# A decoder step: 512-column moving operands in the expert tables, sample tokens' expert rows fetched by index, gates kept in another DRAM order

## The chip, the cores and the metric

The kernel runs on one core of one Trainium2 chip. The core has TensorE (PE, whose weight loads are shown apart as PEld), VectorE (DVE), ScalarE (ACT), GpSimd (POOL), SyncE (SP) and 16 DMA engines. The metric is the device time of one execution in microseconds (us); lower is better. Before the change three runs took 4409.46, 4419.07 and 4418.88 us, median 4418.88 us.

## The reference

A two-layer decoder trunk works on 520 tokens of width 1024 at once: 512 tokens of a prompt and 8 sample tokens (one new token each of 8 sequences). Layer 0 mixes tokens by a gated convolution and attention, layer 1 by a chunked spatial gate. The change is in what follows in each layer, an expert lookup (`_peer`). For each token, 8 heads pick 16 of 16,384 experts by two product keys, which gives 128 experts and 128 gates per token:

```python
q = (xf @ wq).reshape(n, PEER_HEADS, 2, PEER_DK // 2)
s = jnp.einsum('nhpd,hpkd->nhpk', q, keys)
top_s, top_i = lax.top_k(s, PEER_TOPK)               # 16 of 128, for two halves of the key
cand_s = top_s[:, :, 0, :, None] + top_s[:, :, 1, None, :]
cand_i = top_i[:, :, 0, :, None] * PEER_NKEYS + top_i[:, :, 1, None, :]
best_s, pos = lax.top_k(cand_s..., PEER_TOPK)        # 16 of 256
gate = jax.nn.softmax(best_s, axis=-1)
hi = jax.nn.gelu(jnp.einsum('bed,bd->be', jnp.take(u_tab, ei, axis=0), xi))
y  = jnp.einsum('be,bed->bd', gi * hi, jnp.take(v_tab, ei, axis=0))
```

An expert's number is 128 times a first index plus a second index. `u_tab` and `v_tab` have 16,384 rows of 1024 numbers each, 64 MB per table and layer. All numbers are fp32.

## The kernel before, in words

Activations lie with the features on the partitions: `xt`, `res` and the like are [128, 8, 520], feature block by feature block, with the 520 tokens side by side (columns 512 to 519 are the sample tokens).

The expert lookup (`peer`, on each engine a function of that name, called for layer 0 and layer 1) doesn't fetch rows. It multiplies all tokens by both whole tables and lets the gates, which are zero for experts that were not picked, select.

- **First table.** For each of 128 first indices a chunk of 128 experts' u rows (512 KB) is multiplied by all tokens: `chunk` on PE (line 1229; the matmul is line 1241). fp32 accuracy comes from splitting each operand into a rounded part and a remainder (`whi`, `wlo`, `xh`, `xl`, float32r), with three products for each of 8 feature blocks. The 520 columns are done in two matmuls of 260, so a chunk is 48 matmuls. SP loads a chunk into `wraw` (two slots), ACT rounds it (`whi`, line 570), POOL takes the remainder (`wlo`, line 547), PE multiplies, ACT applies the gelu (`hid`, line 696) and SP stores the 128x520 result to DRAM (`hidden`, line 414). The rounding of the next chunk of a slot stands behind the gelu of the present one on ACT, and the gelu waits until the store of that slot's result before has landed (`h_out`).
- **Gates.** Beside the first table the tokens are ranked, 104 at a time (5 token tiles, `topk` on DVE). A tile's gates are then spread out on PE: for groups of 4 tokens DVE builds two one-hot matrices (`one_hots`, lines 1196 and 1199) and PE multiplies them (`gate_group`, line 1434) to a 128x128 table of gates per token. ACT copies it into `gst` (line 710), and SP stores `gst` by half tiles of 52 tokens, each in four pieces of 832 KB (`store_gates`, line 421). `PLAN` says after how many pairs of chunks each tile's work comes, and whether one or two groups of tokens follow each chunk. In DRAM `gates` is [first index, second index, token], so a store writes runs of 52 numbers (208 bytes).
- **Second table.** For each of 32 groups of four first indices, and each of 8 feature blocks (v = 0 to 7), PE adds up `second_table` (line 1490, matmul line 1499): 4 first indices by 3 products by 2 halves, 24 matmuls of 260 columns. The moving operand is `wth`/`wtl`, the rounded part and the remainder of hidden times gate (`gated` on DVE, line 1052; `round_wt` on ACT, line 764; `split_wt` on DVE, line 1056). The weights are `vhi`/`vlo` (ACT line 757, DVE line 1043). DVE adds each result to `res` (`take_v`, line 1064). SP loads the v rows (line 399, four slots), hidden (line 428) and gates (line 429, 260 KB for each first index).

The order on each engine is written out by hand: program order with semaphores. SP issues all loads and stores of both tables from one queue, in the order of the code, and waits there for each one's condition.

The lines most spoken of are these:

```python
for h in range(2):                                              # chunk, line 1239
    mm = e.matmul(pstr[:, slot, h, 0:HALF], w[:, slot, k * P:(k + 1) * P], x[:, k, h * HALF:(h + 1) * HALF], ...)
for h in range(2):                                              # second_table, line 1498
    mm = e.matmul(aux[:, 2 * (v % 2) + h, 0:HALF], w[:, v % 4, j * P:(j + 1) * P], x[:, par, j, h * HALF:(h + 1) * HALF], ...)
```

Of the kernel before, what the change touches and what calls it, by code (L numbers as in the profile page):

```python
# [30 lines left out]
P = 128  # L31
# [21 lines left out]
SUB = 4  # L53
GROUP = 4
# [5 lines left out]
GROUPS = TT // SUB  # L60
EXP_AT = 17
# [19 lines left out]

SMP = {"operands": 0, "bias": 1, "keys": 2, "max": 17, "exp": 19, "norm": 19, "turn": 20, "turned": 20, "values": 21}
# [21 lines left out]
class Steps:  # L104
# [10 lines left out]
    def settle(self):  # L115

        self.engine.wait_ge(self.sem, self.count)

# [10 lines left out]
def trunk(nc, i, o):  # L129
    with ExitStack() as ctx:  # L130
# [81 lines left out]
        choice_end = used[0]  # L212

# [4 lines left out]
        wth = place("wth", [P, 2, GROUP, N], F32R)  # L218
        wtl = place("wtl", [P, 2, GROUP, N], F32R)
        gc = place("gc", [P, GROUP, N], F32)  # L220
        hl = place("hl", [P, GROUP, N], F32)
        wt = place("wt", [P, 2, N], F32)

        hid = place("hid", [P, 2, N], F32, max(used[0], choice_end))
        used[0] = max(used[0], choice_end) + 2 * 4 * N
# [29 lines left out]
        g_in = [sem(f"g_in{n}") for n in range(4)]  # L255
# [69 lines left out]
        v_taken = sem("v_taken")  # L325

# [47 lines left out]
        def _(e):  # L374
# [26 lines left out]
            def peer_tables(layer):  # L401
# [15 lines left out]
                def store_gates(half, part):  # L417

                    n = P // PIECES
                    e.wait_ge(gate_taken, (half + 1 + layer * NT * 2) * subs)  # L420
                    e.dma_start(gates[layer][part * n:(part + 1) * n, :, half * GH:(half + 1) * GH].rearrange("a b n -> b a n"),
                                gst[:, half % 2, part * n:(part + 1) * n, :]).then_inc(gates_out[half % 2], 16)

                def load_h(g, j):
# [4 lines left out]
                    e.dma_start(gc[:, j, :], gates[layer][bass.ds(g * GROUP + j, 1)].rearrange("a p n -> p (a n)")).then_inc(g_in[j], 16)  # L429
# [12 lines left out]
                while pair < P // 2:  # L442
# [4 lines left out]
                    if pair == P // 2 - 3:  # L447

                        for par in range(2):
                            e.wait_ge(gates_out[par], 16 * PIECES * NT * (layer + 1))  # L450
                        for j in range(GROUP):
                            load_h(0, j)
                        for v in range(4):
                            load_v(layer, 0, v)
                    store_h(pair)
# [10 lines left out]
                def period(g, more):  # L466
# [6 lines left out]
                period(0, True)  # L473
                with e.Fori(1, NG - 1) as g:
                    period(g, True)
                period(NG - 1, False)
# [21 lines left out]
        def _(e):  # L498
# [37 lines left out]
            def peer(layer):  # L536
# [6 lines left out]
                with e.Fori(1, P // 2) as p:  # L543
                    for slot in range(2):
# [3 lines left out]
                                        ALU.subtract).then_inc(u_lo, 1)  # L548

# [14 lines left out]
        def _(e):  # L564
# [119 lines left out]
            def peer(layer):  # L684
# [6 lines left out]
                def hidden_one(pair, slot):  # L691
# [4 lines left out]
                    e.activation(halves(hid[:, slot, :]), pstr[:, slot, :, 0:HALF], ACT.Gelu_apprx_tanh).then_inc(chunk_taken, 1)  # L696
# [7 lines left out]
                def take_gates(tt, n):  # L704
# [4 lines left out]
                    e.wait_ge(gate_done, tt * GROUPS + (n + 1))  # L709
# [55 lines left out]

                def period(g, par, more):
                    for v in range(8):
# [4 lines left out]
                        elif more:  # L772
                            round_v(g + 1, v - 6)

# [5 lines left out]
                period(0, 0, True)  # L780
                with e.Fori(0, NG // 2 - 1) as q:
# [28 lines left out]
        def _(e):  # L810
# [213 lines left out]
            def peer(layer):  # L1024
# [3 lines left out]

                for w in range(NT + 1):
                    tt = w + layer * NT  # L1030
                    ranking = topk(tt, Steps(e, topk_step, tt * per), per) if w < NT else iter(())
                    if w:
                        e.wait_ge(pick_taken, tt)
                        for n in range(GROUPS):
                            one_hots((tt - 1) * GROUPS + n, n % 2, n * SUB)
# [9 lines left out]
                def gated(g, j):  # L1045
# [602 lines left out]
```

## Time and profile before

| what | value |
|---|---|
| three runs, median | 4409.46, 4419.07, 4418.88 us; 4418.88 us |
| span of the profiled execution, first to last instruction | 4402.0 us |
| PE busy | 4151.5 us, 94% |
| PEld busy | 3973.3 us, 90% |
| DVE, ACT, POOL busy | 2675.8 us (61%), 1465.7 us (33%), 765.7 us (17%) |
| first-table matmuls, line 1241 | 16,512 (some 12,288 of them in the two first tables) |
| second-table matmuls, line 1499 | 12,288 |
| DMA | 633.66 MB, 144 GB/s on average; 359,736 of 582,347 packets are under 512 bytes |

The page gives no time of the profiled execution beside its span; the runs are 7.5 to 17.1 us longer than it. "Busy" of PE is not work at its peak, since matmuls overlap and their ends are modelled; their starts tell the pace. "Granted clock" is the share of TensorE's full clock in a stretch; 1.00 is 2.4 GHz and 0.50 is 1.2 GHz. In time the execution is: attention and its projections up to about 490 us, the first table of layer 0 to about 1547 us (its gates from 655 us), the second table to about 2295 us, the spatial gate to about 2570 us, and the two tables of layer 1 to about 4373 us.

### The profile page before, as it was taken

To read this page: it belongs to the slowest core of one execution; us is meant where nothing else is said; L and a number is where in the kernel's file an instruction comes from. 1 tells how busy PE (TensorE), PEld (TensorE's weight loads), DVE (VectorE), ACT (ScalarE), POOL (GpSimd) and SP (SyncE) were. 2 spreads that over 40 slices of the span, in tenths; PEclk is the share of its full clock that TensorE was granted. 3 is DMA by queue.
4 is the path that set the end of the run, shared out by engine and by line. 5 is a ranking of instruction groups with operands and counts; after the bars stand their busy time and mean duration, and the time that the engine had idled before them with its cause. 6 is when DMAs were issued, how large, how long until landed. Compare 5 with 4: busy or idle time off the path is not lost.

```text
span 4402.0 us, 85855 instructions
## 1 busy us (share of the span) xinstructions
PE 4151.5 (94%) x32404; PEld 3973.3 (90%) x32404; DVE 2675.8 (61%) x5472; ACT 1465.7 (33%) x2084; POOL 765.7 (17%) x430
## 2 busy tenths in 40 slices
PE   8889999999898899999999999999999989999998
PEld 8635899989898899999999789999999889999998
DVE  2332368787786266666653336868787626666665
ACT  3221333434434322222224233433343432222223
POOL 4111123333232300000001012333333320000000
PEclk9989999999999999999999799999999999999999
DMA  4444235766777955555542023576696786555553
GB/s 120 131 128 139 77 113 133 145 132 139 141 139 137 182 183 184 183 184 184 183 134 74 28 77 113 135 144 135 141 147 146 132 174 193 182 182 183 184 184 112
DMA packets 582347, 633.66 MB, mean 144 GB/s; under 512 B 359736, under 2 KB 359864, under 8 KB 581584
## 3 DMA queue, kind: packets, MB, share of 16 engines
q1 hardware_dynamic: 573760, 608.77, 55.0%
q0 software_dynamic: 8464, 23.38, 1.8%
q8 instruction: 62, 1.02, 0.1%
q14 instruction: 61, 0.50, 0.0%
HBM read 491.36 MB, written 140.66 MB: 144 GB/s over the span
## 4 chain that ended last, share of the span: by engine, by line
PE 49%; issue 39%; POOL 8%; ACT 2%; DVE 2%; DMA 1%; POOLq 0%; SPq 0%; ACTq 0%; DVEq 0%
PE aux L1499 33%; PE pstr L1241 9%; POOL wlo L547 8%; PE pstr L1366 1%; PE pstr L1386 1%; PE aux L1284 1%; PE pstr L1339 1%; PE aux L1546 1%; PE aux L1545 0%; PE aux L1275 0%; DVE rstd L847 0%; PE aux L1319 0%; PE aux L1329 0%; ACT xt L604 0%; PE pstr L1275 0%
## 5 line engine op out<-in xcount | busy, mean ns | idle before, releaser
L1241 PE MATMUL pstr<-xh,whi 128*128 128x260 f32 x5504 | 1155.3, 292 | 114.1 <-POOL wlo L547 86.4
L1241 PE MATMUL pstr<-xh,wlo 128*128 128x260 f32 x5504 | 1124.2, 286 | 0.0
L1241 PE MATMUL pstr<-xl,whi 128*128 128x260 f32 x5504 | 1122.6, 286 | 0.0
L1241 PEld LDWEIGHTS pstr<-xh,whi 128*128 128x128 f32 x5504 | 868.7, 193 | 124.8 <-issue 85.5
L547 POOL TENSOR_TENSOR wlo<-wraw,whi 128x1024 fp32r<-128x1024 f32 x252 | 633.4, 2515 | 1460.6 <-ACT whi L570 1459.1
L1241 PEld LDWEIGHTS pstr<-xl,whi 128*128 128x128 f32 x5504 | 867.6, 193 | 0.0
L1241 PEld LDWEIGHTS pstr<-xh,wlo 128*128 128x128 f32 x5504 | 864.9, 192 | 0.0
L1499 PE MATMUL aux<-wth,vhi 128*128 128x260 f32 x4096 | 827.0, 283 | 7.5 <-DVE res L1064 7.5
L1499 PE MATMUL aux<-wth,vlo 128*128 128x260 f32 x4096 | 826.8, 284 | 0.0
L1499 PE MATMUL aux<-wtl,vhi 128*128 128x260 f32 x4096 | 825.5, 283 | 0.0
L1499 PEld LDWEIGHTS aux<-wth,vhi 128*128 128x128 f32 x4096 | 633.4, 189 | 8.5 <-DVE vlo L1043 7.9
L1199 DVE TENSOR_SCALAR oh<-cst,pickt 128x128 f32<-128x128 f32 x1040 | 637.7, 674 | 0.0
L1499 PEld LDWEIGHTS aux<-wth,vlo 128*128 128x128 f32 x4096 | 632.8, 189 | 0.0
L1499 PEld LDWEIGHTS aux<-wtl,vhi 128*128 128x128 f32 x4096 | 631.2, 189 | 0.0
L1043 DVE TENSOR_TENSOR vlo<-vraw,vhi 128x512 fp32r<-128x512 f32 x512 | 352.1, 688 | 308.9 <-ACT vhi L757 308.9
L764 ACT ACTIVATE wth<-wt 128x520 fp32r<-128x520 f32 x256 | 163.2, 638 | 1025.0 <-DVE wt L1052 1025.0
L696 ACT ACTIVATE hid<-pstr 128x520 f32<-128x520 f32 x256 | 156.5, 611 | 1038.5 <-PE pstr L1241 794.0
L1064 DVE TENSOR_TENSOR res<-res,aux 128x520 f32<-128x520 f32 x512 | 354.6, 693 | 209.1 <-PE aux L1499 209.1
L1196 DVE TENSOR_TENSOR oh<-cst,pickt 128x512 f32<-128x512 f32 x260 | 201.2, 774 | 395.5 <-PE aux L1434 318.3
L570 ACT ACTIVATE whi<-wraw 128x1024 fp32r<-128x1024 f32 x344 | 361.5, 1051 | 122.4 <-PE pstr L1241 86.7
L1434 PE MATMUL aux<-oh,oh 128*128 128x128 f32 x2080 | 282.1, 284 | 41.1 <-ACT gst L710 27.7
L710 ACT ACTIVATE gst<-aux 128x512 f32<-128x512 f32 x260 | 312.7, 1240 | 15.1 <-PE aux L1434 14.9
(194 smaller groups left out, 2906.5 us busy)
## 6 DMA issues: line engine op xcount, KB each, us to landing
wraw<-in_u SPq DMA_DIRECT2D x256, 512.0 KB, 3.8
vraw<-in_v SPq DMA_DIRECT2D x512, 256.0 KB, 2.9
hidden<-hid SPq DMA_DIRECT2D x256, 260.0 KB, 2.2
gates<-gst SPq DMA_DIRECT2D x80, 832.0 KB, 18.5
hl<-hidden SPq DMA_DIRECT2D x256, 260.0 KB, 2.7
gc<-gates SPq DMA_DIRECT2D x256, 260.0 KB, 3.9
wraw<-in_w SPq DMA_DIRECT2D x88, 512.0 KB, 3.5
kv<-in_ck SPq DMA_DIRECT2D x32, 256.0 KB, 3.1
```

The lines of the kernel that those rows point to most:

```text
L547: e.tensor_tensor(wlo[:, slot, :], wraw[:, slot, :], whi[:, slot, :].bitcast(F32), ALU.subtract).then_inc(u_lo, 1)
L570: e.activation(whi[:, slot, :], wraw[:, slot, :], ACT.Copy).then_inc(w_hi, 1)
L696: e.activation(halves(hid[:, slot, :]), pstr[:, slot, :, 0:HALF], ACT.Gelu_apprx_tanh).then_inc(chunk_taken, 1)
L710: e.activation(gst[:, half % 2, :, n % subs * SUB:(n % subs + 1) * SUB].rearrange("p a n -> p n a"), aux[:, n % 2, :].rearrange("p (n a) - ...
L764: e.activation(wth[:, par, j, :], wt[:, j % 2, :], ACT.Copy).then_inc(wt_hi, 1)
L1043: e.tensor_tensor(vlo[:, v % 4, :], vraw[:, v % 4, :], vhi[:, v % 4, :].bitcast(F32), ALU.subtract).then_inc(v_lo, 1)
L1064: e.tensor_tensor(r, r, aux[:, 2 * (v % 2):2 * (v % 2) + 2, 0:HALF], ALU.add).then_inc(v_taken, 1)
L1196: e.tensor_tensor(oh2[:, slot], spread(c(IOTA), 1, shape), spread(pickt[:, 1, at:at + SUB], 2, shape), ALU.is_equal).then_inc(oh_ready, 1)
L1199: e.tensor_scalar(oh1[:, slot, r, :], c(IOTA), pickt[:, 0, at + r:at + r + 1], pickt[:, 2, at + r:at + r + 1], ALU.is_equal, ALU.mult).the ...
L1241: mm = e.matmul(pstr[:, slot, h, 0:HALF], w[:, slot, k * P:(k + 1) * P], x[:, k, h * HALF:(h + 1) * HALF], start=k == 0 and w is whi and x ...
L1434: mm = e.matmul(aux[:, slot, r * P:(r + 1) * P], oh2[:, slot, r, :], oh1[:, slot, r, :], start=True, stop=True)
L1499: mm = e.matmul(aux[:, 2 * (v % 2) + h, 0:HALF], w[:, v % 4, j * P:(j + 1) * P], x[:, par, j, h * HALF:(h + 1) * HALF], start=j == 0 and w ...
```

## The change

The tables' matmuls take the 512 prompt tokens alone, in one matmul of 512 columns in place of two of 260. In the first table a result fills one PSUM bank (`pstr[:, slot, 0, :]`), in the second table `aux[:, v % 2, :]`. `hid`, `hl`, `wt`, `wth`, `wtl` and `hidden` shrink from 520 to 512 columns.

The 8 sample tokens get their experts' rows by index. At the end of the ranking DVE writes the expert numbers and gates of these tokens (`sample_list`). POOL then fetches, for one token after the other, the 128 u rows (one row per partition, 512 KB) and later the 128 v rows, by indirect DMA into a ring of four buffers `rows`. In the groups g = 1 and 2 of the second table PE spreads a token's activations over all partitions (`sample_spread`) and DVE multiplies them with the rows and adds up (`sample_dot`). In the groups 3 and 4 PE multiplies the v rows with gate times gelu (`sample_values`), and DVE adds the sum to `res` (`sample_add`). Groups 0 to 4 are therefore written out, and the loop over the rest starts later.

`gates` in DRAM becomes [half tile, second index, first index, token]: a store writes, for each partition, 32 first indices by 52 tokens in one run (6,656 bytes). The gates of four first indices are loaded at once, double-buffered by group, in 10 runs of 832 bytes per partition, and `gated` becomes two multiplications, of 468 and of 44 columns.

```diff
-        gates = [nc.dram_tensor(f"gates{n}", (P, P, N), F32, kind="Internal").ap() for n in range(DEPTH)]
-        hidden = [nc.dram_tensor(f"hidden{n}", (P, P, N), F32, kind="Internal").ap() for n in range(DEPTH)]
+        gates = [nc.dram_tensor(f"gates{n}", (2 * NT, P, P, GH), F32, kind="Internal").ap() for n in range(DEPTH)]
+        hidden = [nc.dram_tensor(f"hidden{n}", (P, P, SEQ), F32, kind="Internal").ap() for n in range(DEPTH)]
...
-                    e.dma_start(gates[layer][part * n:(part + 1) * n, :, half * GH:(half + 1) * GH].rearrange("a b n -> b a n"),
-                                gst[:, half % 2, part * n:(part + 1) * n, :]).then_inc(gates_out[half % 2], 16)
+                    e.dma_start(gates[layer][half, :, part * n:(part + 1) * n, :].rearrange("b a n -> b (a n)"),
+                                gst[:, half % 2, part * n:(part + 1) * n, :].rearrange("b a n -> b (a n)")).then_inc(gates_out[half % 2], 16)
...
-                    e.dma_start(gc[:, j, :], gates[layer][bass.ds(g * GROUP + j, 1)].rearrange("a p n -> p (a n)")).then_inc(g_in[j], 16)
+                def load_gates(g, par):
+                    if layer or not isinstance(g, int) or g > 1:
+                        e.wait_ge(g_used, g * GROUP + (layer * P - GROUP))
+                    e.dma_start(gc[:, par, :, :], by_group[bass.ds(g, 1)].rearrange("a b h c -> b (a h) c")).then_inc(g_in[par], 16)
...
+                for j in range(2 * DEC):
+                    table, t = (i["ur"], j) if j < DEC else (i["vr"], j - DEC)
+                    if RING <= j < RING + DEC:
+                        e.wait_ge(s_dot, layer * DEC + j - RING + 1)
+                    elif j >= RING + DEC:
+                        e.wait_ge(s_value, layer * DEC + j - RING - DEC + 1)
+                    e.indirect_dma_start(rows[:, j % RING, :], None, table,
+                                         bass.IndirectOffsetOnAxis(ap=s_id[:, t:t + 1], axis=0)).then_inc(rows_in[j % RING], 16)
...
+                def sample_dot(t):
+                    e.wait_ge(rows_in[t % RING], 16 * (2 * DEC // RING * layer + t // RING + 1))
+                    e.wait_ge(s_spread, layer * DEC + t + 1)
+                    row = rows[:, t % RING, :]
+                    e.scalar_tensor_tensor(row, row, 1.0, pstr[:, 0, :, :].rearrange("p a n -> p (a n)"), ALU.mult, ALU.mult,
+                                           accum_out=s_dots[:, t:t + 1]).then_inc(s_dot, 1)
...
+                        if first in C_U:
+                            mm = e.matmul(pstr[:, slot, 0, :], w[:, slot, k * P:(k + 1) * P], x[:, k, 0:SEQ],
+                                          start=k == 0 and w is whi and x is xh, stop=k == KB - 1 and w is wlo)
+                            continue
...
-                            for h in range(2):
-                                mm = e.matmul(aux[:, 2 * (v % 2) + h, 0:HALF], w[:, v % 4, j * P:(j + 1) * P],
-                                              x[:, par, j, h * HALF:(h + 1) * HALF],
+                            mm = e.matmul(aux[:, v % 2, :], w[:, v % 4, j * P:(j + 1) * P], x[:, par, j, :],
...
+                def sample_spread(t):
+                    if t == 0:
+                        e.wait_ge(s_rows, 3 * (layer + 1))
+                    if t or layer:
+                        e.wait_ge(s_dot, layer * DEC + t)
+                    for h in range(2):
+                        for n in range(2):
+                            mm = e.matmul(pstr[:, 0, h, :], pickr[:, t:t + 1].to_broadcast([DEC, P]), xr[:, n, h * 512:(h + 1) * 512],
+                                          start=n == 0, stop=n == 1)
+                    mm.then_inc(s_spread, 1)
+
+                def sample_values(t):
+                    if t == 0:
+                        e.wait_ge(s_weight, layer + 1)
+                    j = DEC + t
+                    e.wait_ge(rows_in[j % RING], 16 * (2 * DEC // RING * layer + j // RING + 1))
+                    for k in range(KB):
+                        at = k * DEC + t
+                        mm = e.matmul(aux[:, 2, at:at + 1], rows[:, j % RING, k * P:(k + 1) * P], s_w[:, t:t + 1], start=True, stop=True)
+                    mm.then_inc(s_value, 1)
...
+                        if DOTS_G <= g < DOTS_G + 2 and v % 2 == 0:
+                            sample_spread((g - DOTS_G) * 4 + v // 2)
+                        if g == VALS_G and v >= 2:
+                            sample_values(v - 2)
+                        if g == VALS_G + 1 and v < 2:
+                            sample_values(v + 6)
```

The next rows are SP's queue where a layer's first table ends and its second begins, before the change (`wraw` is a chunk of u, `hl` and `gc` the hidden values and gates of a first index, `vraw` a block of v rows).

```order
L421 DMA gates<-gst 128x32x52 x2
L414 DMA hidden<-hid 128x520 x2
L382 DMA wraw<-in_u 128x1024 x2
L428 DMA hl<-hidden 128x520
L429 DMA gc<-gates 128x520
...
L399 DMA vraw<-in_v 128x512 x4
L414 DMA hidden<-hid 128x520 x2
```

After the change the same place on SP reads:

```order
L452 DMA gates<-gst 128x1664 x2
L445 DMA hidden<-hid 128x512 x2
L413 DMA wraw<-in_u 128x1024 x2
L466 DMA gc<-gates 128x10x208
L459 DMA hl<-hidden 128x512 x4
L430 DMA vraw<-in_v 128x512 x4
L466 DMA gc<-gates 128x10x208
L445 DMA hidden<-hid 128x512 x2
```

The stores of gates stand where they stood, with one run per partition; two loads of four first indices' gates take the place of four loads of one, the second of them ahead of the store of hidden values.

The next rows are DVE in the second table before the change, two feature blocks of a group (`wt` is hidden times gate, `vlo` a remainder of v, `res` the sum that takes PE's result).

```order
L1064 TENSOR_TENSOR res<-res,aux 128x520
L1052 TENSOR_TENSOR wt<-hl,gc 128x520
L1043 TENSOR_TENSOR vlo<-vraw,vhi 128x512
L1064 TENSOR_TENSOR res<-res,aux 128x520
L1056 TENSOR_TENSOR wtl<-wt,wth 128x520
L1043 TENSOR_TENSOR vlo<-vraw,vhi 128x512
```

After the change, in group 1:

```order
L1170 TENSOR_TENSOR res<-res,aux 128x512
L1155 TENSOR_TENSOR wt<-hl,gc 128x468
L1157 TENSOR_TENSOR wt<-hl,gc 128x44
L1144 TENSOR_TENSOR vlo<-vraw,vhi 128x512
L1170 TENSOR_TENSOR res<-res,aux 128x512
L1115 SCALAR_TENSOR_TENSOR rows,s_dots<-rows,pstr 128x1024
L1162 TENSOR_TENSOR wtl<-wt,wth 128x512
L1144 TENSOR_TENSOR vlo<-vraw,vhi 128x512
```

The product with the gates is split in two in every group; the instruction of line 1115 stands behind every second feature block of groups 1 and 2 only.

## Rows read from the trace of the kernel before

**Rows 1.** Page, the chain that ended last, by line.

```profile
PE aux L1499 33%; PE pstr L1241 9%; POOL wlo L547 8%; PE pstr L1366 1%; PE pstr L1386 1%; PE aux L1284 1%; PE pstr L1339 1%; PE aux L1546 1%; PE aux L1545 0%; PE aux L1275 0%; DVE rstd L847 0%; PE aux L1319 0%; PE aux L1329 0%; ACT xt L604 0%; PE pstr L1275 0%
```

**Rows 2.** Stretches: busy us (count) by engine, granted clock, DMA share, GB/s.

```profile
1800.00:1900.00 100.00, 100.00 (x834) 100.00 (x834) 66.40 (x104) 28.64 (x52) 0.00 (x0) 1.00 0.58 186
...
883.24:949.44 66.20, 66.20 (x563) 66.20 (x561) 55.37 (x133) 24.57 (x28) 21.91 (x9) 1.00 0.67 135
...
655.19:1556.41 901.22, 828.31 (x6718) 823.58 (x6717) 632.73 (x1474) 347.27 (x397) 288.45 (x114) 0.96 0.73 143
...
2744.80:3638.33 893.53, 824.47 (x6718) 819.89 (x6717) 623.17 (x1474) 346.92 (x397) 284.78 (x114) 0.96 0.73 144
...
1135.09:1182.18 47.09, 36.23 (x250) 35.38 (x249) 38.28 (x53) 19.15 (x20) 13.14 (x5) 0.86 0.55 111
```

**Rows 3.** Timeline of PE at half clock: start, us, what, count.

```profile
977.73 0.64 PE L1241 MATMUL pstr<-xh,whi 128*128 128x260 f32 x2
...
978.16 0.64 PE L1241 MATMUL pstr<-xl,whi 128*128 128x260 f32 x2
```

**Rows 4.** Timeline of PEld, fp32 matmuls of 512 columns, full clock granted.

```profile
250.11 0.14 PEld L1366 LDWEIGHTS pstr<-kv,qd 128*64 128x64 f32 x1 [0.29 <-issue]
...
250.54 0.14 PEld L1366 LDWEIGHTS pstr<-kv,qd 128*64 128x64 f32 x1 [0.29 <-issue]
```

**Rows 5.** Timeline of PE, fp32 matmuls of 260 columns, each in two passes.

```profile
2294.68 2.79 PE L1275 MATMUL pstr<-res,cst 128*128 128x260 f32 x12
```

**Rows 6.** Waits of PE in the whole span: us in total, times, longest.

```profile
PE pstr L1241 <- POOL wlo L547: 86.4, 22, 6.4
...
PE aux L1434 <- ACT gst L710: 27.7, 10, 4.2
...
PE aux L1434 <- DVE oh L1199: 13.2, 5, 4.8
```

**Rows 7.** Timeline of SP's queue at two stores of gates.

```profile
943.60 11.98 SPq L421 DMA_DIRECT2D gates<-gst  x2
```

**Rows 8.** Timeline of ACT and PE after it; idle before in brackets.

```profile
968.56 1.28 ACT L696 ACT_TABLE_LOAD   x1 [11.02 <-DMA hidden<-hid]
...
976.27 0.79 PE L1241 MATMUL pstr<-xh,whi 128*128 128x260 f32 x2 [6.37 <-POOL wlo L547]
```

**Rows 9.** DMA issues: count, KB each, median us to landing.

```profile
gates<-gst SPq DMA_DIRECT2D x80, 832.0 KB, 18.5
...
hidden<-hid SPq DMA_DIRECT2D x256, 260.0 KB, 2.2
...
vraw<-in_v SPq DMA_DIRECT2D x512, 256.0 KB, 2.9
...
kv<-in_cv POOLq DMA_DIRECT2D x32, 256.0 KB, 3.2
```

**Rows 10.** Timeline of DVE and ACT over two feature blocks of the second table.

```profile
1702.42 0.69 DVE L1064 TENSOR_TENSOR res<-res,aux 128x520 f32<-128x520 f32 x1 [0.75 <-PE aux L1499]
...
1703.04 0.69 DVE L1052 TENSOR_TENSOR wt<-hl,gc 128x520 f32<-128x520 f32 x1
...
1703.76 0.64 ACT L764 ACTIVATE wth<-wt 128x520 fp32r<-128x520 f32 x1 [4.11 <-DVE wt L1052]
...
1704.31 1.14 ACT L757 ACTIVATE vhi<-vraw 128x512 fp32r<-128x512 f32 x2
...
1704.96 0.69 DVE L1043 TENSOR_TENSOR vlo<-vraw,vhi 128x512 fp32r<-128x512 f32 x1 [1.23 <-ACT vhi L757]
...
1705.56 0.69 DVE L1064 TENSOR_TENSOR res<-res,aux 128x520 f32<-128x520 f32 x1
...
1706.17 0.69 DVE L1056 TENSOR_TENSOR wtl<-wt,wth 128x520 fp32r<-128x520 f32 x1
```

**Rows 11.** Timeline of PE, fp32 matmuls with 4 columns and full weights.

```profile
400.17 1.95 PE L1415 MATMUL aux<-cab,om 128*128 128x4 f32 x16 [1.37 <-DVE om L1014]
```

**Rows 12.** Costliest groups: a DVE pass over 1024 columns that reads PSUM.

```profile
L1014 DVE TENSOR_TENSOR om<-pstr,cab 128x1024 f32<-128x1024 f32 x1 | 1.2, 1225 | 29.0 <-PE pstr L1386 29.0
```

More of the change, by code:

```diff
@@ L254, in trunk @@
         v_in = [sem(f"v_in{n}") for n in range(4)]
-        g_in = [sem(f"g_in{n}") for n in range(4)]
+        g_in = [sem(f"g_in{n}") for n in range(2)]
         h_out = [sem(f"h_out{n}") for n in range(2)]
@@ L325, in trunk @@
         v_taken = sem("v_taken")
+        s_listed = sem("s_listed")
+        s_turned = sem("s_turned")
+        s_rows = sem("s_rows")
+        rows_in = [sem(f"rows_in{n}") for n in range(RING)]
+        s_spread = sem("s_spread")
+        s_dot = sem("s_dot")
+        s_gelu = sem("s_gelu")
+        s_weight = sem("s_weight")
+        s_value = sem("s_value")
         ws_masked = sem("ws_masked")
@@ L471, in period @@
                             load_h(g + 1, v // 2)
[L473 to L476, printed above, removed]
+                        if gates_too and v == 1:
+                            load_gates(g + 2, par)
+                period(0, 0, True)
+                with e.Fori(0, NG // 2 - 2) as q:
+                    period(q * 2 + 1, 1, True)
+                    period(q * 2 + 2, 0, True)
+                period(NG - 3, 1, True)
+                period(NG - 2, 0, True, False)
+                period(NG - 1, 1, False, False)
             load_stage(C_AB, N_AB, i["w"], 0, None)
@@ L548, in peer @@
                                         ALU.subtract).then_inc(u_lo, 1)
+                for par in range(2):
+                    e.wait_ge(gates_out[par], 16 * PIECES * NT * (layer + 1))
+                e.wait_ge(s_listed, layer + 1)
+                for j in range(2 * DEC):
[6 more added lines that the diff above has]
+                                         bass.IndirectOffsetOnAxis(ap=s_id[:, t:t + 1], axis=0)).then_inc(rows_in[j % RING], 16)
             peer(0)
@@ L779, in peer @@
                 hidden_pair(P // 2 - 1)
-                period(0, 0, True)
-                with e.Fori(0, NG // 2 - 1) as q:
+                for g in range(VALS_G + 2):
+                    period(g, g % 2, True)
+                with e.Fori((VALS_G + 1) // 2, NG // 2 - 1) as q:
                     period(q * 2 + 1, 1, True)
@@ L1506, in period @@
                         second_table(g, v, par)
-                period(0, 0)
-                with e.Fori(0, NG // 2 - 1) as q:
+                        if not isinstance(g, int):
+                            continue
+                        if (g, v) == (0, 4):
+                            sample_turn()
+                        if DOTS_G <= g < DOTS_G + 2 and v % 2 == 0:
+                            sample_spread((g - DOTS_G) * 4 + v // 2)
[3 more added lines that the diff above has]
+                            sample_values(v + 6)
+                for g in range(VALS_G + 2):
+                    period(g, g % 2)
+                with e.Fori((VALS_G + 1) // 2, NG // 2 - 1) as q:
                     period(q * 2 + 1, 1)
```

124 lines of the change are left out of this document (96 added, 28 removed).

## The prediction, made before the changed kernel ran

> **What bounds the kernel now.** I read the chain of waits first: the second table's matmuls alone are 33% of the span on it, and the first table's, of which the profile puts most down to "issue", make up the larger part of the rest [rows 1]. So PE is the engine to look at, and the stretches tell how. In the second table PE is busy all the time at a granted clock of 1.00 and starts 834 matmuls of 260 columns in 100 us, 119.9 ns each, while DVE is busy 66% and DMA 58% [rows 2]. That is PE's own pace. In the first table a clean stretch of ten groups gives 563 matmul records in 66.20 us, 117.6 ns each. But the two whole stretches with gates hold 6718 records in 901.22 and 893.53 us at a mean clock of 0.96 [rows 2]. At the clean pace 6718 records are 790 us, so 111 and 104 us, 215 in all, are waits and the half clock that follows them.
>
> The waits are mostly of one kind: 86.4 us in 22 waits for POOL's remainder of u, and 27.7 us for ACT's copy of gates [rows 6]. One of them, step by step: SP is held 11.98 us by two stores of gates [rows 7]; the store of hidden values stands behind them, ACT sits idle 11.02 us until it has landed, the rounding of the next chunk stands behind that on ACT, and PE idles 6.37 us for POOL [rows 8]. A store of gates takes 18.5 us to land where 260 KB of hidden values take 2.2 us [rows 9].
>
> **One matmul of 512 columns for two of 260.** 260 columns at 2.4 GHz are 108.3 ns, and the measured pace is 119.9. At half clock two starts lie 0.43 us after the two before [rows 3], which is 217 ns each, 260 columns at 1.2 GHz with nothing on top. So the extra 11.6 ns are no fixed price of an instruction at every clock. Two explanations are left: something beside the stream (the load of 128 weight columns) takes about 120 ns and no longer hides, or the stream of float32r at full clock can't go faster. fp32 records of 512 columns start 430 ns apart [rows 4], which is two cycles a column at 2.4 GHz (426.7 ns) and 3 ns, and 12 of 260 columns (216.7 ns of stream, full weights) take 2.79 us, about 219 ns apart once the last one's 382 ns, its group's mean in the trace, are taken off [rows 5]. In both, the weights hide behind a stream of over 200 ns and 2 to 3 ns are left. A float32r matmul of 512 columns streams 213.3 ns with the same weights. I take 216 ns. The ends are 213.3 (nothing on top) and 235.8 (the pace per column of now, 119.9 x 512 / 260); I choose the value nearest to the fp32 rows, since their stream is as long and hides the same load.
>
> The Trainium skill, "TensorE: Matmul & The Clock Gate", section "Back-to-back issue gap", gives N / 2.4 + 2.5 ns for a warm matmul, an estimate of 216 at 512 columns. By the same rule 260 columns would take 111, and the row says 120; the miss of 9 ns is why I don't hold the 216 for certain. The page also names about 131 ns per matmul at N = 512 as sustained; 512 columns at 2.4 GHz are 213 ns, and no run here shows such a pace.
>
> First table: 256 chunks go from 48 x 119.9 = 5.76 us to 24 x 216 = 5.18, saving 0.57 us each, 146 us. Second table: 512 tiles go from 24 x 119.9 = 2.88 to 12 x 216 = 2.59, saving 0.285 each, 146 us. Sum 292 us.
>
> Is PE still last in the second table? DVE and ACT pass a chain through two feature blocks: sum into res at 1702.42, product with the gates, ACT's two roundings, remainder of v, next sum at 1705.56, which is 3.14 us; then three more DVE steps of 0.61 us, 1.83 [rows 10]. That is 4.97 us against 5.76 of PE. After the change the product is two instructions (I add 0.14 us for the second start, taking both ends of 0 to 0.35), and 8 fewer columns in four steps take 0.03 off: 5.08 against 2 x 2.59 = 5.18. PE stays last by 0.1 us. With 0.35 the chain would be 5.29 and cost 0.11 x 256 = 28 us. DMA moves the same 4.2 MB or so per group in 20.7 us in place of 23, so a share of 58% becomes about 65%; SP's loads run four blocks ahead and land in 2.9 us [rows 9], so I count nothing for the shorter runs of the gates' loads.
>
> **Gates in one run per partition.** A store goes from 4096 runs of 208 bytes to 128 runs of 6,656 bytes. Loads with 128 runs of 2,048 bytes land in 2.9 us [rows 9]; four times the bytes should land in 4 to 8 us and hold SP for less than a microsecond. Then the hidden store is no longer late, and neither are ACT, POOL and PE. What is late next is DVE. In the clean stretch it is busy 55.37 of 66.20 us, 5.54 per group [rows 2]; PE's cycle falls from 6.62 to 5.18 + 0.87 = 6.05, so DVE just keeps up. At a token tile's end, where the ranking's large steps fall, it doesn't: from 1135.09 to 1182.18 DVE is busy 38.28 us for eight groups and four chunks [rows 2], which PE would do in 4 x 5.18 + 8 x 0.87 = 27.7. Two of a layer's tiles have such an end (two groups after each chunk): 10.6 us and some 2 us of half clock each, 25 us. I give the two other tiles 7 us together, and 12 us to the boundaries between tiles and to the step into the second table, where hidden values still have to land. So 44 us a layer stay of 107, and 127 us go in both layers. The ends: nothing goes (0) and all goes (215).
>
> **The fetched sample tokens.** PE gains work in the second table, per layer: 16 transposes at about 0.11 us, 32 matmuls of 512 columns at 0.216, and 64 fp32 products with one column, two passes each. Sixteen such records with 4 columns take 1.95 us with the last one's tail [rows 11], 0.113 apart, so 128 take 14.5 us. Sum 1.8 + 6.9 + 14.5 = 23 us, 46 in both layers. DVE gains eight passes over 1024 columns, which take about 1.2 us [rows 12]; in groups 1 and 2 its chain is then 6.3 us for two blocks against PE's 5.18 + 0.87, 0.25 x 8 = 2 us a layer. I add 1 us a layer for the first wait of ACT and PE on each other: 6 us in all. The 32 fetches of 512 KB are costed at nothing on PE: the first four of a layer are issued before the second table starts, and the later ones have four blocks of lead, 4 x (2.59 + 1.8) = 17.6 us in groups 3 and 4. POOL's loads of 256 KB took 3.2 us to land [rows 9]; twice the bytes, 6.4 us. If that cover is gone PE waits, see below. From 0 to 17 us a fetch are the bounds I see.
>
> **Sum.** 292 + 127 - 52 = 367 us. The profiled execution's span of 4402.0 becomes 4035. The median of the runs is 16.9 us over that span, so about 4052, and I forecast 4055 us.
>
> **The rivals.**
> Contention for weights (the 9 ns of excess stay on every matmul, 225 ns): 12,288 x 9 = 111 us less gain, 4165 us. For it speaks that the float32r pace of 119.9 is 9 ns over what fp32 shows on top of its stream; against it, that at 1.2 GHz there is no excess.
> The stream is the limit (235.8 ns): 243 us less; the longer chunks then give DVE back about 10, so 4290 us. For it: float32r reads a column per cycle, which no fp32 row does. Against: nothing but the fp32 rows, which read at half that rate.
> DVE's tile ends are hidden (it runs up to two groups ahead): up to 75 us more gain, 3980 us.
> The stores of gates stay slow, because 832 KB and not the 208-byte runs are what holds SP: the change doesn't do that part, 127 us less, 4180 us. Against it speaks that 512 KB of v rows as two loads land in a few us [rows 9].
> Slower than before: the fetches are exposed. POOL needs long for a fetch of 128 rows while DVE works, and PE stands in order at a product whose rows have not come. To eat 367 us the 32 fetches must each hold PE 11.5 us; with 17.6 us of lead, one would have to take 29 us from its release to its landing, and the time would be 4420 or more. POOL's loads at 3.2 us speak against it. The Trainium skill, "SBUF — State Buffer", section "Who interferes with whom", says that a DMA issued by GpSimd waits while DVE, in some of its modes, holds their shared port; its loads here ran while DVE was less busy than in the second table, so this row doesn't refute it.
>
> **How the numbers follow.** Forecast 0.55, its own range 4005 to 4130 (the chain's 28 us, half of the stalls' bounds, 219 ns for a matmul); contention 0.20; stream 0.10; DVE hidden 0.10; stores slow 0.02; fetches exposed 0.03. A range of 3985 to 4235 leaves out the stream, the exposed fetches and half of "DVE hidden", 0.18. A change below 0.3% (13 us) couldn't be told from none. All cases but the exposed fetches end far below 4406: faster 0.96, same 0.01, slower 0.03.
>
> **What would show it.** In the second table 463 records of 512 columns per 100 us (216 ns); 444 or 424 would be the rivals. No wait over 10 us of ACT for hidden values; waits for POOL gone but for a few us, and the longest waits of PE in the first table those for DVE's one-hots at the ends of the third and fourth token tile. Stores of gates landing under 8 us. A granted clock of 0.98 or more in the first tables. The fetches landing under 10 us, and no wait of PE for them. I would be wrong if the second table's tile took over 2.75 us, if PE still waited for POOL some 20 times, or if lines of the sample tokens cost PE over 40 us a layer.

## The result and the profile after

The changed kernel took 4198.13 us (median of 4 runs, 4193.99 to 4209.97), and the kernel before, on the same chip in the same session, 4414.17 us: ratio 0.9526, 95% interval 0.9503 to 0.9549. It is faster, as forecast, and its time lies in the range of 3985 to 4235 us, but 143 us above the 4055 us of the forecast. On another chip the gap was smaller: there the unedited change took 4199.09 us and the kernel before 4364.14 us, ratio 0.9631 (0.9606 to 0.9656). The change takes the same on both; it is the kernel before that differs.

The profiled execution of the change has a span of 4193.8 us against 4402.0, 208 us less. Its stretches, to be laid beside [rows 2] (columns as there):

```profile
1800.00:1900.00 100.00, 100.00 (x442) 82.84 (x441) 70.77 (x129) 31.04 (x54) 0.00 (x0) 1.00 0.59 190
...
644.85:1457.31 812.46, 792.92 (x3979) 664.45 (x3980) 638.75 (x1499) 347.69 (x398) 298.66 (x119) 0.99 0.48 162
2627.55:3440.28 812.73, 793.23 (x3980) 664.70 (x3980) 638.92 (x1499) 347.69 (x398) 298.30 (x119) 0.99 0.48 162
```

In the second table PE still has no gap and the clock is whole, but there are 442 matmuls in 100 us where I expected 463. The first table's stretch with gates fell from 901 and 894 us to 812 and 813, with the granted clock up from 0.96 to 0.99 and the DMA share down from 0.73 to 0.48. So the stalls went, and the matmuls are what came out dearer. Their starts say by how much; first the second table, then the first (start, us, instruction):

```profile
1799.80 0.39 PE L1617 MATMUL aux<-wth,vhi 128*128 128x512 f32 x1
...
1802.06 0.39 PE L1617 MATMUL aux<-wtl,vhi 128*128 128x512 f32 x1
```

```profile
663.11 0.40 PE L1356 MATMUL pstr<-xh,wlo 128*128 128x512 f32 x1
...
665.91 0.39 PE L1356 MATMUL pstr<-xh,wlo 128*128 128x512 f32 x1
```

The first pair is ten matmuls apart, 2.26 us. Over a whole table the starts stand 226.6 ns apart. The second pair is twelve apart, 2.80 us, 233 ns; the mean spacing within the first tables' chunks is 232.6. The forecast had 216 for both. All other signs that the prediction named came as expected. PE's waits (total, times, longest; beside [rows 6]):

```profile
PE aux L1553 <- DVE oh L1314: 19.2, 8, 4.0
...
PE pstr L1356 <- POOL wlo L591: 11.9, 6, 3.1
...
PE aux L1617 <- DVE res L1170: 7.1, 3, 3.5
...
PE aux L1553 <- ACT gst L767: 0.9, 4, 0.2
```

The 22 waits for POOL are 6, none over 3.1 us, and DVE's one-hots now lead. DMA issues and SP's queue, beside [rows 7, 9]:

```profile
gates<-gst SPq DMA_DIRECT2D x80, 832.0 KB, 7.1
gc<-gates SPq DMA_DIRECT2D x64, 1040.0 KB, 5.5
hidden<-hid SPq DMA_DIRECT2D x256, 256.0 KB, 2.1
...
rows<-in_ur,s_id POOLq DMA_INDIRECT x16, 5.3
rows<-in_vr,s_id POOLq DMA_INDIRECT x16, 4.6
```

```profile
906.18 0.90 SPq L452 DMA_DIRECT2D gates<-gst  x2
```

Two stores hold SP 0.90 us instead of 11.98, and a store lands in 7.1 us instead of 18.5; it is still 832 KB, so the rival that the size holds SP falls. The fetches of sample rows land in 5.3 and 4.6 us, and no wait of PE names them.

### The profile page after: what moved, and what is told of

Same layout as the page of the kernel before. It is cut to its first block and busy times, and to the rows that moved or that the text cites. A ratio compares the mean times of both kernels' runs of the same rounds, so it can differ in the third digit from the quotient of the medians.

```text
span 4193.8 us, 61594 instructions
## 1 busy us (share of the span) xinstructions
PE 4040.5 (96%) x20468; PEld 3334.9 (80%) x20468; DVE 2710.7 (65%) x5770; ACT 1478.5 (35%) x2092; POOL 814.5 (19%) x462
## 5 line engine op out<-in xcount | busy, mean ns | idle before, releaser
L1356 PE MATMUL pstr<-xh,whi 128*128 128x512 f32 x2048 | 832.7, 407 | 12.0 <-POOL wlo L591 11.9
L1356 PE MATMUL pstr<-xh,wlo 128*128 128x512 f32 x2048 | 814.9, 398 | 0.0
L1617 PE MATMUL aux<-wth,vhi 128*128 128x512 f32 x2048 | 805.0, 393 | 7.1 <-DVE res L1170 7.1
L1356 PE MATMUL pstr<-xl,whi 128*128 128x512 f32 x2048 | 809.8, 395 | 0.0
L1617 PE MATMUL aux<-wth,vlo 128*128 128x512 f32 x2048 | 799.1, 390 | 0.0
L1617 PE MATMUL aux<-wtl,vhi 128*128 128x512 f32 x2048 | 798.7, 390 | 0.0
L1356 PEld LDWEIGHTS pstr<-xh,whi 128*128 128x128 f32 x2048 | 388.7, 190 | 95.0 <-issue 15.1
L1356 PEld LDWEIGHTS pstr<-xh,wlo 128*128 128x128 f32 x2048 | 387.8, 189 | 92.1
L1356 PEld LDWEIGHTS pstr<-xl,whi 128*128 128x128 f32 x2048 | 388.9, 190 | 84.6
L1170 DVE TENSOR_TENSOR res<-res,aux 128x512 f32<-128x512 f32 x512 | 350.1, 684 | 135.1 <-PE aux L1617 133.3
```

The costliest lines, as they stand in the source:

```text
L1170: e.tensor_tensor(r, r, aux[:, v % 2, :], ALU.add).then_inc(v_taken, 1)
L1356: mm = e.matmul(pstr[:, slot, 0, :], w[:, slot, k * P:(k + 1) * P], x[:, k, 0:SEQ], start=k == 0 and w is whi and x is xh, stop=k == KB - ...
L1617: mm = e.matmul(aux[:, v % 2, :], w[:, v % 4, j * P:(j + 1) * P], x[:, par, j, :], start=j == 0 and w is vhi and x is wth, stop=j == GROUP ...
```

## The experiments

Times are medians. Several chips were used; the change took 4198 and 4199 us on the two where it ran unedited, and where two kernels are compared across chips, the text says so.

**The gates' layout alone**, on the kernel before, with 260-column matmuls and sample columns kept (stores shown; the loads, not shown, take four first indices at once):

```diff
-e.dma_start(gates[layer][part*n:(part+1)*n, :, half*GH:(half+1)*GH]..., gst[...])
+e.dma_start(gates[layer][half, :, part*n:(part+1)*n, :].rearrange("b a n -> b (a n)"), gst[...])
```

> The kernel before with only the gates' layout of the change (stores in one run per partition, loads for four first indices); 260-column matmuls and sample columns stay. Theory: the waits of PE that hang on the stores go, 127 us by the prediction, 135 to 140 us by what is left of the change's 208 us when 125 us of shorter matmuls and 50 to 57 us of sample work are taken out of it: 4275 to 4290 us, 0.968 to 0.971 of before. Rival (the stalls were bounded by PE's own pace and DVE, and the shorter matmuls gave what was gained): 80 us or less, 0.98 or above.

4266.51 us (4260.37 to 4269.57) against 4360.33 for the kernel before on that chip: 94 us less, 0.9784 (0.9755 to 0.9813). Its waits and landing:

```profile
PE aux L1448 <- DVE oh L1213: 23.9, 10, 3.8
...
PE pstr L1255 <- POOL wlo L560: 9.7, 6, 2.6
```

```profile
gates<-gst SPq DMA_DIRECT2D x80, 832.0 KB, 7.2
```

The ratio lies between the two bands and settles nothing, and the time is 9 us under the theory's 4275 to 4290: the kernel before is 54 us faster on this chip than where it was profiled, so the sums don't carry over. The mechanism is shown: with only the layout changed, the waits for POOL fall from 22 to 6 (and the next run, on this same chip, has 22 of them with the old layout).

**The reverse: the change with the old layout.**

```diff
-gates (2*NT, P, P, GH), gc per four first indices
+gates (P, P, N), gc[:, j, :] per first index, 0:SEQ
```

> The changed kernel with the gates' layout of before (208-byte runs, loads per first index), 512-column matmuls and fetched sample rows kept. Theory: PE waits for POOL come back, some 20 waits and 80 to 110 us, and the time is 4198 + 127 to 140 = 4325 to 4338 us, 0.980 to 0.983 of before. Rival (with fewer, longer matmuls a late store costs no more than before per store, but DVE's lag hides part of it): 4260 to 4290 us, 0.965 to 0.972.

4320.29 us (4310.18 to 4323.47), 121 us over the 4199.09 of the change on another chip, where the kernel before takes nearly as long (4364 us, here 4360). That is 5 us under the band of 4325 to 4338 us, and 0.990 of before, outside both bands.

```profile
PE pstr L1341 <- POOL wlo L581: 70.5, 22, 6.0
...
PE aux L1538 <- ACT gst L757: 16.5, 9, 3.0
```

```profile
929.41 10.53 SPq L452 DMA_DIRECT2D gates<-gst  x2
```

The 22 waits for POOL are back, 70.5 us where 80 to 110 were expected, with SP held for 10.53 us by two stores. With 512 columns the layout is worth 121 us, with 260 it was 94; that a shorter chunk leaves a late store less cover is my reading, and no run tests it. Turned round: without the layout, the wider matmuls and the fetched samples together gain only 40 us on this chip (4360.33 to 4320.29), so the gains of the two parts of the change don't simply add up.

**The change without the sample tokens' expert work.**

```diff
-sample_list() / indirect_dma_start(rows...) / sample_turn, _spread, _dot, _weights, _values, _add
```

> The changed kernel without the sample tokens' part of the expert tables (no fetch of rows, no dots, no products with the fetched rows, nothing added to the sample columns): their share of the output is left out. Theory: PE loses 16 transposes, 32 matmuls of 512 columns and 128 one-column records a layer, 25 us, and the few us of waits around them: 50 to 57 us in both layers, 4141 to 4148 us, 0.939 to 0.941 of before. Rival (the sample work stands where PE would have waited for DVE and ACT): 25 us or less, 0.946 or above.

4147.98 us (4146.10 to 4165.90): 51 us under the change (4199.09, another chip), against the 52 us of the prediction. The work is on the path at about its full price. Rows of the change show one of its pieces, 16 products with one column, and that the table's next matmul starts 1.71 us after the first of them, with no wait between:

```profile
3539.91 1.84 PE L1649 MATMUL aux<-s_w,rows 128*128 128x1 f32 x16
3541.62 0.48 PE L1617 MATMUL aux<-wth,vhi 128*128 128x512 f32 x1
```

**What makes a matmul of 512 columns cost 226.6 ns?** Two runs change one thing, or two, in each table:

```diff
 # first run: layer 0, both tables: 32 weight columns; layer 1: row 0 of x throughout, 384 columns
+mm = e.matmul(pstr[0:cols, ...], w[:, slot, k*P:k*P+cols], x[:, row, 0:SEQ], ...)
+mm = e.matmul(aux[0:cols, v%2, 0:n], w[:, v%4, j*P:j*P+cols], x[:, par, j, 0:n], ...)
 # second run: weight block 0 throughout, and row 0 in layer 1; second table 256 columns, then 64 partitions
+mm = e.matmul(pstr[:, slot, 0, :], w[:, slot, 0:P], x[:, row, 0:SEQ], ...)
+mm = e.matmul(aux[:, v%2, 0:n], w[0:rows_, v%4, j*P:(j+1)*P], x[0:rows_, par, j, 0:n], ...)
```

> The changed kernel; in layer 0 both tables use 32 weight columns in place of 128 (32 output features of 128 are computed), in layer 1 the first table's matmuls all read row 0 of x in place of row k, and the second table's stream 384 columns of 512. The outputs of the tables are partial by that. Theory (the load of 128 weight columns is what is left uncovered, 13 ns over the 213.3 of the stream): with 32 columns the spacing falls to 213 to 218 ns in both tables, the first table's extra 6 ns with it. Rival 1 (the stream pays by column): spacing stays 226.6 with 32 weight columns, 384 columns take 170 ns. Rival 2 (a fixed price of an instruction): stays with 32 weight columns, 384 columns take 160 + 13.3 = 173.3 ns. For the first table's 232.5 against 226.6: if the place of the moving row does it, row 0 throughout gives one even spacing in layer 1; if not, the pattern of 227 to 238 ns by position stays.

> The changed kernel; the first table's matmuls take weight block 0 throughout (layer 0), and weight block 0 with row 0 of x (layer 1); the second table streams 256 columns in layer 0, and in layer 1 contracts over 64 partitions of 128. The tables' outputs are partial by that. Rate by column: 256 columns take 113.3 ns; fixed price: 106.7 + 13.3 = 120; a weight load that no longer hides: about 120 as the 260-column matmuls of before. 64 partitions: a theory of reads from the buffer says less than 226.6, the others the same. First table: if weights' and row's addresses meet, the pattern is even in layer 1 and changed in layer 0; if it is the instruction's place in its chunk, it stays in both.

Starts in the second table. 32 weight columns and 512 streamed (ten apart, 2.32 us, 232 ns); 384 streamed (nine apart, 1.56 us, 173.3 ns), both of the first run:

```profile
1799.77 0.39 PE L1619 MATMUL aux<-wth,vhi 128*32 128x512 f32 x1
...
1802.09 0.39 PE L1619 MATMUL aux<-wtl,vhi 128*32 128x512 f32 x1
...
3899.74 0.34 PE L1619 MATMUL aux<-wth,vlo 128*128 128x384 f32 x1
...
3901.30 0.34 PE L1619 MATMUL aux<-wth,vlo 128*128 128x384 f32 x1
```

256 streamed (six apart, 0.72 us, 120 ns), and 512 over 64 partitions at half clock (six apart, 2.56 us, 426.7 ns), of the second run:

```profile
1802.74 0.28 PE L1619 MATMUL aux<-wtl,vhi 128*128 128x256 f32 x1
...
1803.46 0.28 PE L1619 MATMUL aux<-wtl,vhi 128*128 128x256 f32 x1
...
3899.72 0.62 PE L1619 MATMUL aux<-wth,vhi 64*128 64x512 f32 x1
...
3902.28 0.62 PE L1619 MATMUL aux<-wth,vhi 64*128 64x512 f32 x1
```

A quarter of the weight columns made nothing shorter, so the load of weights is not what stays uncovered. Over 1/2.4 ns a column, 256 columns have 13.3 ns on top, 384 have 13.3 and 512 have 13.3: a fixed price of each float32r matmul, neither a share per column nor a load that hides behind a longer stream. At half clock it is gone (512 / 1.2 is 426.7), as with the 260 columns of [rows 3]. The height doesn't matter either: in the first tiles with 64 partitions, still at full clock, the starts stood 226.7 ns apart. One figure doesn't fit to the nanosecond: the 260 columns of the kernel before had 11.6 ns on top, not 13.3, and no run shows why.

The second run is much longer, 4773.90 us, because of its last part:

```profile
3500.00:4100.00 600.00, 600.00 (x1463) 462.40 (x1463) 220.14 (x392) 92.13 (x167) 4.89 (x5) 0.50 0.32 104
```

With 64 of 128 partitions contracted the clock was granted at 0.50 for the whole of 600 us, while PE was busy throughout. It fell 13.6 us into the table and stayed there to the table's end. I hadn't expected that; it is told again below.

The same runs show the second table's floor. Where PE streams only 384 columns, PE waits for DVE, and DVE and ACT, which mostly wait for each other there, set the pace:

```profile
3700.00:3800.00 100.00, 85.76 (x468) 80.12 (x467) 73.19 (x137) 32.92 (x57) 0.00 (x0) 1.00 0.63 207
```

468 matmuls of 12 a tile in 100 us are 2.56 us a tile, 5.13 for two; the prediction worked out 5.08.

**Why the first table pays 6 ns more.** My first theory was the start of every other row of x at 32 bytes off a multiple of 64:

```diff
-xh = place("xh", [P, KB, N], F32R)
+xh = place("xh", [P, KB, N + 8], F32R)      # xl likewise
```

> The changed kernel with the rows of xh and xl padded from 2080 to 2112 bytes, so that every row starts at a multiple of 64 bytes as the second table's rows do. Theory (row starts): the first table's matmuls of 512 columns take 232.5 ns in place of the second table's 226.6 because every other row of x starts 32 bytes off; then both tables go at 226.6, 6144 x 5.9 ns = 36 us less, 0.944 of before against 0.953 of the change. Rival (the place of the weights, or of the instruction in its chunk): the spacing in a chunk stays 227 to 238 ns by position, mean 232.5, and the time stays at 0.953. The 32-column matmuls of the other stages read the same rows and should show the same sign.

4203.75 us (4196.65 to 4206.02), no gain. Twelve matmuls of its first table still take 2.78 us, 232 ns:

```profile
661.40 0.39 PE L1357 MATMUL pstr<-xh,wlo 128*128 128x512 f32 x1
...
664.18 0.40 PE L1357 MATMUL pstr<-xh,wlo 128*128 128x512 f32 x1
```

That theory fell. But the pattern of short and long spacings within a chunk had moved, so the rows' places did matter. In the two runs above the pattern was the same within a nanosecond with weight block 0 throughout (mean 232.6), and with row 0 throughout it settled at 227 after ten matmuls (mean 228.3). So it is the moving rows, not which weight block is loaded. The next run sets the distance between them:

```diff
+at = k * 512 if first == C_U[0] else k % 7 * 576          # 2048 or 2304 bytes, before 2080
+mm = e.matmul(pstr[...], w[...], x[:].rearrange("p a n -> p (a n)")[:, at:at + SEQ], ...)
+at = j % 3 * 520 if layer == 0 else j * SEQ               # second table: 2080 bytes, before 2048
```

> The changed kernel with the moving rows taken at other distances in the same tensors: in the first table the k-th row starts at 2048 k bytes in layer 0 and at 2304 (k mod 7) bytes in layer 1, in place of 2080 k; in layer 0's second table the rows start at 2080 (j mod 3) bytes in place of 2048 j. The tables' values are wrong by that. Theory (the distance from one moving row to the next makes the first table's spacing uneven): at 2048 bytes layer 0's first table goes at 227 ns from the tenth matmul of a chunk on, as with row 0 throughout, mean 227 to 228 against 232; layer 0's second table becomes uneven, 229 to 234 in place of 226.6; 2304 bytes tell which distances are even. Rival (the chunk's start behind the gate group's products of 128 columns, and 24 matmuls in place of 12, make it): nothing changes in either table.

In layer 0's first table twelve spacings of a chunk's later half now take 2.72 us, 226.7 ns, and the mean is 228.3 in both layers, so with either distance; in the second table of layer 0, with 2080 bytes, ten take 2.32 us, 232 ns:

```profile
665.42 0.39 PE L1357 MATMUL pstr<-xh,wlo 128*128 128x512 f32 x1
...
668.14 0.40 PE L1357 MATMUL pstr<-xh,wlo 128*128 128x512 f32 x1
...
1799.69 0.39 PE L1619 MATMUL aux<-wtl,vhi 128*128 128x512 f32 x1
...
1802.01 0.40 PE L1619 MATMUL aux<-wth,vlo 128*128 128x512 f32 x1
```

The tables swapped their prices with their distances. That is shown. The rival keeps a small part: behind a gate group's products of 128 columns the first ten spacings of a chunk stay uneven, 224 to 236 ns, even at 2048 and 2304 bytes, while a chunk with no group before it goes at 227 from its start. The run as a whole took 4196.14 us (one run), hardly less: layer 0's second table lost about 14 us by its spacing, the first tables won about 26, and the waits for DVE's one-hots grew from 19.2 to 25.4 us.

**A better order of the gates.** The longest waits left beside the gates, 4 us each, are at the third and fourth tile's ends, where two groups follow each chunk; and DVE idles before the first groups, since PE comes to them later than the ranking ends:

```profile
644.83 2.62 DVE L1311 TENSOR_TENSOR oh<-cst,pickt 128x512 f32<-128x512 f32 x1 [12.53 <-ACT pickt L800]
```

```diff
-PLAN = [(6,0,0), (0,11,1), (0,11,1), (0,9,2), (0,9,2), (0,1,6)];  TAIL = 5
+PLAN = [(5,0,0), (0,11,1), (0,11,1), (0,11,1), (0,11,1), (0,1,6)];  TAIL = 4
```

> The changed kernel with another table of work: five pairs of chunks before the first groups in place of six, no chunk with two groups at the ends of the third and fourth token tile, four pairs after the last group in place of five. Theory (DVE's ranking holds PE at those ends, and PE's first groups have 12.5 us of lead to spare): the waits of 4.1 to 4.3 and 0.9 to 1.4 us at the two ends of each layer become one of 1.75 each, 4 x 3.7 = 15 us and some 4 to 8 us of half clock after them less, 0.995 of the change. Rival (DVE is as late whatever chunk the groups stand behind, since it has the same work between two tiles): the waits move to the last tile, where two groups follow each chunk, and the time stays within 5 us.

> The changed kernel itself, unedited, beside the others on their chip. 4190 to 4210 us.

4187.53 us (4184.67 to 4189.00) against 4199.09 (4195.45 to 4207.19) on the same chip: 11.6 us less, 0.997 of the change where the theory had 0.995 (19 to 23 us) and the rival 5 us at most. The waits at the tiles' ends went, but SP now waited 7.0 us for the last gates, a store of hidden values stood behind that, and PE waited 9.8 us for POOL (views: SP's, ACT's and PE's waits at the end of layer 0's first table):

```profile
SPq L487 <- DMA gates<-gst: 7.0, 1, 7.0
```

```profile
ACT hid L753 <- DMA hidden<-hid: 13.8, 1, 13.8
```

```profile
PE pstr L1356 <- POOL wlo L591: 9.8, 1, 9.8
```

It is the chain of [rows 8] again, at one place. Padding the rows to 2176 bytes beside it, a multiple of 128, gave next to nothing:

> The changed kernel with the table of work of the run with five pairs before the first groups, and rows of xh and xl padded to 2176 bytes, a multiple of 128. If rows that start at the same place modulo 128 are even, the first table's mean falls from 232 to 227 or 228, 6144 x 4.5 = 28 us less than that run's 4187.5: 4160 us. If 128 is not enough, 4185 to 4190 us, as with 2112 bytes.

4181.91 us (4181.57 to 4190.30, another chip), mean spacing 232.0 ns: near the second case, that 128 is not enough. Then the wait was moved one pair of chunks later, and, on top of that, the rows put 2304 bytes apart:

```diff
-if pair == P // 2 - 3:
+if pair == P // 2 - 2:
```

```diff
+PAD = 56        # and tv, ti, tif of the ranking live in the columns between the rows
```

> The run with five pairs before the first groups, and with the second table's first loads (and SP's wait for the stores of gates ahead of them) one pair of chunks later, at pair 62 of 64. In that run SP waited 7.0 us for the last gates with the hidden stores behind it, and PE stood 9.8 us for POOL once a layer. Theory: that wait goes or falls to about 3 us as in the change, 2 x 7 = 14 us less, 4174 us. Rival (the second table's first products of gates come later by as much): within 4 us of 4187.5.

> The same with rows of xh and xl at 2304 bytes, a multiple of 256 (three small tables of the ranking live in the columns between the rows, so that it fits). Theory: the first table's matmuls go evenly at 227 ns from the tenth of a chunk on, mean 227.4 against 232, 6144 x 4.6 = 28 us less than the run beside it: 4146 us. Rival (the ranking on DVE is then what PE waits for, since its cycle falls by 0.11 us a chunk): half of it, 4160 us.

4166.55 us (4165.04 to 4167.81) with the wait moved: 21 us under the run with the new order, on another chip (about 14 were expected), and the 9.8 us wait is gone; the longest for POOL is 2.4 us. 4141.75 us (4138.29 to 4149.42) with the rows as well, on the same chip: 24.8 us less where 28 were expected. Twelve spacings of its first table, 2.72 us:

```profile
664.16 0.39 PE L1359 MATMUL pstr<-xh,wlo 128*128 128x512 f32 x1
...
666.88 0.40 PE L1359 MATMUL pstr<-xh,wlo 128*128 128x512 f32 x1
```

This version beats both kernels: 0.9492 (0.9471 to 0.9513) of the kernel before on its chip, and 57 us under the 4199.09 of the change on another chip.

## Why the prediction was right in kind and 143 us low

- **PE bounds the kernel.** Right. PE is busy all of the second table, and the sample work, when left out, came off the time at its full price.
- **One matmul of 512 columns for two of 260.** This is the step that failed, where the text says "I take 216 ns" and chooses "the value nearest to the fp32 rows, since their stream is as long and hides the same load". First table: 24 x 232.6 = 5.58 us a chunk against 5.76, 44 us in 256 chunks. Second: 12 x 226.6 = 2.72 us a tile against 2.88, 81 us in 512. Together 125 us where 292 were counted, 167 us missing. The reason was wrong too: "two explanations are left" skipped a third, a fixed price that comes with a float32r stream at full clock. [Rows 3] had only excluded a fixed price at every clock, and the fp32 rows that I leaned on stream half a column per 1/2.4 ns, as a float32r matmul does at half clock; they couldn't show it. Nor do they all hide "the same load": the rows of [rows 4] load 64 weight columns.
- **The rivals of that step.** Contention for weights had nearly the right size (225 ns, 444 matmuls in 100 us where 442 came), and 4165 us came within 33 us of the result, but 32 weight columns showed its mechanism to be wrong. That the stream is limited per column is excluded by 120, 173.3 and 226.6 ns, which have the same 13.3 on top; its 235.8 was itself a slip for 236.1 (119.9 x 512 / 260). By the Trainium skill, "TensorE: Matmul & The Clock Gate", section "Back-to-back issue gap", the estimate is 216 ns at 512 columns; the trace has 226.6, so the measurement decides against it here.
- **DVE and ACT in the second table.** Right: 5.13 us for two tiles against 5.08.
- **Gates in one run.** Right. Landing 7.1 us (4 to 8 expected, from "four times the bytes", which are 3.25 times: 832 KB against 256), SP free after 0.9, waits for POOL 6 instead of 22, longest waits those for one-hots at the third and fourth tile's ends, 4.0 us, so these are not hidden as one rival had it. No wait of ACT for hidden values exceeds the 7.1 us of this row:

```profile
ACT hid L753 <- DMA hidden<-hid: 14.1, 2, 7.1
```

  Of the 208 us gained, 125 came from matmuls and 51 were spent on the sample work; that leaves 134 for the stalls, where 127 were counted. This is a remainder, not a measurement: the three kinds of waits of [rows 6] fell from 127.3 to 32.0 us, 95 less, and the layout alone was measured at 94 us, on a chip where the kernel before is faster.
- **Sample tokens.** Right: 51 us against 52. The fetches are hidden, so the slower rival falls. POOL waited 156.9 us for DVE to be done with a buffer, as the ring of four is programmed; whether a transfer under way ever waits for DVE, as that rival had it, no run here shows.
- **The sum.** 167 us of missing matmul gain, less 7 of stalls and 1 of sample work, is 159 us of span. I had also added 20 us for what lies around the span; the median lies only 4 us over the profiled span here. 159 - 16 = 143. That addition was a misreading: in every run where both are known, the time is 1.6 to 1.9 us over the span, so the 16.9 us before were mostly a profiled execution faster than the median, and the slip hid 16 us of the miss. The result lies outside the forecast's own 4005 to 4130 us; that the wider range holds it is owed to the rival of contention, right in size by luck and wrong in mechanism.

## What to carry to other kernels

A price read from one pace is not a model: before counting on a wider operand, take the pace at two widths in the same data type and at the same clock, since a fixed price and a slow stream look alike at one. When a store in short runs is late, follow what is queued behind it: one queue's 10 us became PE's wait through three engines, twice in this study. And look at the distance between the rows of a moving operand: 224 bytes of padding a row were worth 25 us.

## What the runs showed of the hardware

- A float32r matmul at full clock takes 13.3 ns over its columns' 1/2.4 ns, with 256, 384 and 512 columns, and with 64 partitions as with 128; at half clock nothing. The 260 columns of the kernel before took 11.6. Why is open.
- For 512 columns that holds with moving rows 2048 or 2304 bytes apart, but for some ten matmuls behind a group of 128-column products. At 2080, 2112 and 2176 bytes the spacing is uneven, some 225 to 238 ns by position, mean 231 to 233. With 32 weight columns it was uneven (mean 232) at 2048 too; that stays unexplained.
- Contracting over 64 partitions instead of 128, with PE busy throughout, went with a granted clock of 0.50 (1.2 GHz) for 600 us on end, where the full height ran at 1.00 (100 us of the change's second table). One run shows it.
- The kernel before takes 4414 us on some chips and 4360 to 4365 on others, while the change takes 4198 and 4199. As the gates' layout is what cost the most stalls, the short runs may be what differs: with the old layout in the changed kernel, on a chip where the kernel before takes 4360 us, a store of gates landed in 17.3 us, against 18.5 in the profile of the kernel before. That is a hint from two different kernels; only a profile of the kernel before on the other chips would show it.
